# Two heads of 64 features in the two column halves of one array pass: probabilities scaled beforehand, gates turned instead of outputs

## What is computed

```python
p = jax.nn.softmax(s, axis=-1).astype(v.dtype)      # swa: with a learned sink among the logits
out = jnp.einsum('bhqs,bhsd->bhqd', p, v)           # d = 64
y = jnp.concatenate([ya * jax.nn.silu(ga), yb * jax.nn.silu(gb)], axis=-1)
x = x + y @ w_out_ab[j]
```

## Time and profile before

| | |
|---|---|
| median of 3 runs | 951.78 us (950.68 to 952.01) |
| the profiled execution, its own time | 951.7 us |
| its span in the trace | 949.9 us |
| PE busy | 936.1 us, 99% |
| PEld busy | 815.5 us, 86% |
| DVE busy | 637.9 us, 67% |
| ACT busy | 544.1 us, 57% |
| granted clock of PE over the span | 0.998 |

### The profile page before, as it was taken

One profiled execution on the slowest core, in us unless ns is written; L12 is line 12 of the kernel. 1 busy time (PEld: TensorE's weight loads), 2 busy tenths in 40 slices (PEclk: granted clock), 3 DMA queues, 4 the chain that ended last, 5 costly groups with the idle time before them and its releaser, 6 DMA issues.

```text
span 949.9 us, 14440 instructions
## 1 busy us (share of the span) xinstructions
PE 936.1 (99%) x5452; PEld 815.5 (86%) x5452; DVE 637.9 (67%) x1258; ACT 544.1 (57%) x1046; POOL 57.2 (6%) x109
## 2 busy tenths in 40 slices
PE   9999999999999999999999999999999999999997
PEld 7778788888888898989888888899988898888886
DVE  4888784877776667667666656477964767556664
ACT  6686673657676575567444444465754666444442
POOL 3001330002010030000000000000000000000000
PEclk9999999999999999999999999999999999999999
DMA  9986534554334274445556656665455256655641
GB/s 286 260 194 121 175 133 158 181 181 146 136 121 113 77 211 161 149 130 173 187 179 198 200 177 233 183 184 153 139 173 177 89 178 189 204 183 179 201 175 44
DMA packets 109584, 159.88 MB, mean 168 GB/s; under 512 B 10734, under 2 KB 45900, under 8 KB 109260
## 3 DMA queue, kind: packets, MB, share of 16 engines
q1 hardware_dynamic: 109080, 158.40, 53.7%
q10 hardware_dynamic: 436, 0.56, 0.2%
HBM read 156.32 MB, written 2.11 MB: 167 GB/s over the span
## 4 chain that ended last, share of the span: by engine, by line
PE 92%; DVE 3%; ACT 1%; issue 1%; DMA 1%; SPq 1%; DVEq 0%; ACTq 0%
PE bank L498 22%; PE bank L500 22%; PE bank L499 22%; PE bank L1206 9%; PE bank L1209 5%; PE bank L640 3%; PE bank L654 2%; PE bank L666 2%; PE bank L552 2%; DVE w_lo L1970 1%; DMA raw<-in_w_in_ab 1%; PE bank L625 1%; PE bank L1347 1%; SPq L2759 1%; DVE xT L2028 0%
## 5 line engine op out<-in xcount | busy, mean ns | idle before, releaser
L1970 DVE TENSOR_TENSOR w_lo<-raw,w_hi 128x1024 fp32r<-128x1024 f32 (+3 forms) x296 | 335.2, 1177 | 136.6 <-ACT w_hi L1425 136.1
L1425 ACT CAST w_hi<-raw 128x1024 fp32r<-128x1024 f32 (+3 forms) x296 | 282.1, 1011 | 128.2 <-DMA raw<-in_mlp_w_in 72.0
L498 PE MATMUL bank<-w_hi,xT 128*128 128x512 f32 (+1 forms) x366 | 145.2, 397 | 1.4 <-issue 0.9
L500 PE MATMUL bank<-w_hi,xT 128*128 128x512 f32 (+1 forms) x366 | 141.2, 386 | 0.0
L499 PE MATMUL bank<-w_lo,xT 128*128 128x512 f32 (+1 forms) x366 | 140.9, 385 | 0.0
L498 PE MATMUL bank<-w_hi,hT_hi 128*128 128x512 f32 (+1 forms) x348 | 136.7, 393 | 2.0 <-DVE w_lo L1970 1.7
L500 PE MATMUL bank<-w_hi,hT_lo 128*128 128x512 f32 (+1 forms) x348 | 135.0, 388 | 0.0
L499 PE MATMUL bank<-w_lo,hT_hi 128*128 128x512 f32 (+1 forms) x348 | 134.9, 388 | 0.0
L498 PE MATMUL bank<-xT,w_hi 128*128 128x256 f32 x368 | 106.0, 288 | 0.3 <-DVE w_lo L1970 0.3
L1206 PE MATMUL bank<-xT,w_hi 128*128 128x512 f32 x384 | 104.5, 394 | 0.0
L500 PE MATMUL bank<-xT,w_lo 128*128 128x256 f32 x368 | 104.1, 283 | 0.0
(11 more groups left out here) (276 smaller groups left out, 1313.7 us busy)
## 6 DMA issues: line engine op xcount, KB each, us to landing
raw<-in_mlp_w_in SPq DMA_DIRECT2D x32, 1024.0 KB, 5.2
raw<-in_mlp_w_out SPq DMA_DIRECT2D x32, 1024.0 KB, 5.1
raw<-in_w_in_ab SPq DMA_DIRECT2D x13, 1024.0 KB, 10.6
raw<-in_w_in_cd SPq DMA_DIRECT2D x13, 1024.0 KB, 5.1
raw<-in_xa_w_kv SPq DMA_DIRECT2D x8, 1024.0 KB, 5.1
raw<-in_sb_w_qkv SPq DMA_DIRECT2D x16, 512.0 KB, 5.0
raw<-in_w_out_ab SPq DMA_DIRECT2D x4, 1024.0 KB, 5.2
raw<-in_w_out_cd SPq DMA_DIRECT2D x4, 1024.0 KB, 5.1
```

Of the source, the lines that this page charges most:

```text
L498: pe.matmul(o, wh, ih, start=start, stop=False, skip_group_check=True)
L500: return pe.matmul(o, wl, ih, start=False, stop=stop, skip_group_check=True)
L1425: nc.scalar.copy(w_hi[:, u % SLOTS, a], raw[:, u % SLOTS, a]).then_inc(hi_ready, 1)
L1970: V.tensor_tensor(w_lo[:, u % SLOTS, a], raw[:, u % SLOTS, a], w_hi[:, u % SLOTS, a].bitcast(F32), ALU.subtract).then_inc(lo_ready, 1)
```

## The change

In moba, fox and swa, DVE scales the exponentials by the reciprocal of their sum in place (`normalise`, two instructions on 128 x 128 and 128 x 256 behind the reciprocal), and `turn_probs` waits for that (`norm_ready`) and no longer for the exponentials alone. `values_pair` replaces two calls of `values`: v (128 x 64) is the stationary operand, the turned probabilities are the moving one (256 and then 128 columns), and the two heads of a pair are placed in the column halves of the array by `tile_position`, so that one bank holds features by tokens for both. It stands once at the end of an iteration. The gates are turned instead of the outputs (`turn_gate`, 8 transposes for each of ga, gb and gd, the same number as before): ga at the end of fill 1 into banks 3 and 7, gb at the end of fill 11 into banks 0 and 1, gd at the start of fill 3 of swa into banks 0 and 3. ACT copies the first of the two banks back to SBUF, DVE the second (`turned_gate`). `outputs` is now one product on 128 x 256 for a pair, and ACT and DVE split its result from SBUF (`gated_hi`, `gated_lo`).

```diff
+            def values_pair(ka, kb):
+
+                g = ka["g"]
+                begin(("Y", g), 7)
+                pe.wait_ge(probsT_ready, kb["turn"])
+                places = ((ka, 0), (kb, HD))
+                for k, a in places:
+                    pe.matmul(banks[7][a:a + HD, 0:S], k["v"](0), k["pt"][:, 0:S], start=True, stop=False, tile_position=(0, a),
+                              skip_group_check=True)
+                for k, a in places:
+                    ins = pe.matmul(banks[7][a:a + HD, P:S], k["v"](1), k["pt"][:, S:S + P], start=False, stop=True, tile_position=(0, a),
+                                    skip_group_check=True)
+                end(("Y", g), ins, (gated_ready, pair_no[ka["kind"]] + ka["h"] // 2 + 1))
+                products["Y", kb["g"]] = products["Y", g]
+
+            def turn_gate(name, bs):
+
+                panel = panel_of[name]
+                for t in range(T):
+                    for one in released[name, t]:
+                        pe.wait_ge(*one)
+                for n, b in enumerate(bs):
+                    begin(("gT", name, n), b)
+                    for c in (2 * n, 2 * n + 1):
+                        for t in range(T):
+                            o = banks[b][:, (c % 2) * S + t * P:(c % 2) * S + (t + 1) * P]
+                            ins = pe.transpose(o, arena[:, panel, t * PANEL + c * P:t * PANEL + (c + 1) * P], ident[:, :])
+                    end(("gT", name, n), ins)
...
                     for n in range(2):
-                        old = ks[2 * p - 2 + n] if p else None
                         if p:
-                            turn_probs(old)
+                            turn_probs(ks[2 * p - 2 + n])
                         for f in fill.get(2 * p + n, []):
                             f()
-                        if p:
-                            values(old)
...
+                    if p:
+                        values_pair(*ks[2 * p - 2:2 * p])
...
+            def turned_gate(name):
+
+                condition(act, ("gT", name, 1))
+                ps = condition(act, ("gT", name, 0))
+                nc.scalar.copy(pan(panel_of[name], 0), ps[:, :]).then_inc(read_of(("gT", name, 0))[0], 1)
+                own.last = read_of(("gT", name, 0))
...
             def outputs(k):
 
-                recip(k)
-                g, vd = k["g"], k["vd"]
-                ps = condition(dve, ("Y", g))
-                for t in range(T):
-                    o = k["gate"](t)
-                    ins = V.scalar_tensor_tensor(out=o, in0=ps[:, t * vd:(t + 1) * vd], scalar=rsum[:, 2 * g + t:2 * g + t + 1],
-                                                 in1=o, op0=ALU.mult, op1=ALU.mult)
-                    own.sig(ins, y_ready if t == T - 1 else None)
+                o = gated_chunk(k["kind"], k["h"] // 2)
+                ps = condition(dve, ("Y", k["g"]))
+                dve.wait_ge(*read_of(("gT", {"moba": "ga", "fox": "gb", "swa": "gd"}[k["kind"]], k["h"] // 4)))
+                own.sig(V.tensor_tensor(o, ps[:, 0:S], o, ALU.mult), gated_ready)
...
-                0: [lambda: gate_finish("ga")], 1: [qk_squares("qb")], 2: [qk_rsqrt("qb")],
+                0: [lambda: gate_finish("ga")], 1: [qk_squares("qb")], 2: [qk_rsqrt("qb"), lambda: turned_gate("ga")],
```

More of the change, by code:

```diff
@@ L395, in build @@
             turns += not first_map
-            outputs += k["kind"] in ("moba", "fox", "swa") or k["kind"] == "diff" and k["c"] == 1
-            norms += k["kind"] in ("mla", "xa") or k["kind"] == "diff" and k["c"] == 1
+            outputs += k["kind"] == "diff" and k["c"] == 1
+            norms += k["kind"] in ("moba", "fox", "swa", "mla", "xa") or k["kind"] == "diff" and k["c"] == 1
             k.update(turn=turns, output=outputs, norm=norms)
@@ L454, in build @@
         row_rope = pan(11, 0)[:, S:2 * S]
-        GATE_PARTS = ((0, 2, 4, 3), (2, 1, 5, 5), (3, 1, 6, 7))
+        gate_panel_of = {"moba": 3, "fox": 7, "swa": 6}
+        gated_chunk = lambda kind, p: arena[:, gate_panel_of[kind], p * S:(p + 1) * S]
+        pair_no = {kind: 4 * n for n, kind in enumerate(("moba", "fox", "swa"))}
+        panel_of = {"qa": 0, "ka": 1, "va": 2, "ga": 3, "qb": 4, "kb": 5, "vb": 6, "gb": 7,
+                    "qc": 0, "kc": 1, "vc": 2, "gc": 3, "qd": 4, "kvd": 5, "gd": 6}
         block = ctx.enter_context(nc.Block())
@@ L646, in turn_probs @@
                 begin(("PT", g), b)
-                if k["kind"] in ("moba", "fox", "swa", "sb"):
+                if k["kind"] == "sb":
                     pe.wait_ge(probs_ready, g + 1)
@@ L891, in gate, with gate_chunks @@
                 yr[key] = gated(key, *a)
-            def gate_part(key, panel, n, ks):
-                first, chunks, b0, last = GATE_PARTS[n]
-                yr[key, n] = gated((key, n), panel, b0, ks[last]["output"], first, chunks)
+            def gate_chunks(key, chunks):
+                yr[key] = chunks_ready(state["loT"])
+                state["loT"] += chunks
             def gate_chunk(key):
@@ L1475, in hi_one, with gated_hi @@
                 own.sig(ins, hiT_ready)
+            def turned_gate(name):
[3 more added lines that the diff above has]
+                own.last = read_of(("gT", name, 0))
+            def gated_hi(kind, ps, base):
+                for p in ps:
+                    act.wait_ge(gated_ready, pair_no[kind] + p + 1)
+                    own.sig(nc.scalar.copy(xT_hi[:, base + p, :], gated_chunk(kind, p)), hiT_ready)
             def hi_T(name, chunks, dst, base=0):
@@ L1662, in _, with pairs @@
             front("qa", "ka", "va", "ga")
-            def pairs(ks, units_at, after, ahead={}, both_turned=()):
+            def pairs(ks, units_at, after, ahead={}):
                 for p in range(len(ks) // 2 + 1):
@@ L2313, in _, with pairs @@
             front("qa", "ka", "va", "ga")
-            def pairs(ks, after, late, between={}, early=()):
+            def pairs(ks, after, late, between={}):
                 for p in range(len(ks) // 2 + 1):
```

86 lines of the change are left out of this document (47 added, 39 removed).

## The result

The changed kernel takes 959.41 us (median of 6 runs, 958.15 to 960.1) where the kernel before takes 951.27 in the same series: a ratio of 1.0081, 95% interval 1.0070 to 1.0091 (the two medians alone give 1.0086). The profiled execution took 959.21 with a span of 957.4, so 7.5 more than the one before (951.7 and 949.9). The forecast was 958.4, within 954 to 964.

What follows compares the result with a forecast made beforehand. PE, busy 99% of the span, was taken to bound the kernel, with DVE and ACT mattering only where PE waits. From 951.7 us, -3.2 + 1.7 + 5.1 + 1.1 + 2.0 = +6.7 gave 958.4, range 954 to 964.

Steps and rivals of the forecast that it cites:

- values, 12 pairs: Values of two heads on PE: overlapping column halves cost 0.96 a pair instead of 1.22, saving 3.2 us over twelve.
- first wait, gate: Turning ga after fill 1: PE idles until DVE finishes the gate, about 69.2; +1.7 us.
- bank 3: 13th matmul of kb: PE waits from 74.1 to 79.2 for ACT's copy, behind head 2's exponentials; +5.1 us.
- clock: PE's clock falls to half in the 5.1 us wait and takes time to return; +2.0 us, bounds 0 and 2.7.
- later waits: Rest of the pairs and swa: 2.4 us of new waits less 1.3 given back; +1.1, bounds -2.1 and +3.5.
- the other end of the bound, 1.6: Cost in us of a pair of values if the column halves run one after the other.
- Rival 2: Column halves of the values run serially or overlap only partly: 965 us, or 961; chance 0.20.
- Rival 3: PE does not wait for bank 3, ACT's copy being over by 74.1: 951.3 us, no change; chance 0.07.
- Rival 1: PE's clock holds through the long wait: 956.4 us; chance 0.15.
- 1.3 given back: Part of PE's three longest earlier idle times in the pairs, 2.1 us together, that shrinks because PE comes later.
- Nothing on the path except where named: DVE's extra scaling and pair products, 6.6 us, were claimed to delay nothing beyond the named waits.
- Rival 4: DVE's chain sets the pace at 103 to 126, so the 5.1 us wait melts to about 2: 955; chance 0.08.

Runs made afterwards that it cites:

- e4: Changed kernel with both heads of a pair in the same column half, one after the other, second head's values left out; 965.69 us, ratio 1.0147.
- e1: Changed kernel with the two banks of turned ga swapped, so VectorE's early copy reads bank 3 and ScalarE's late one bank 7; 953.37 us, ratio 1.0018.
- e6: On top of e1, copies of turned gb and gd and the high parts of moba's and fox's outputs moved on ScalarE; 952.85 us, ratio 1.0005.
- e8: Changed kernel, banks as they were, with ScalarE's copy of bank 3 moved ahead of the exponentials of head 2; 953.09 us, ratio 1.0014.
- e2: Changed kernel with ga's banks swapped and ga turned in fill 2, behind the scores, instead of at the end of fill 1; 953.41 us, ratio 1.0017.
- e9: e7 with the 48 scalings of the probabilities left out on VectorE, so outputs lack the division by the sums; 948.22 us, ratio 0.9966.
- e5: Changed kernel with head 0 scaled before gate ga is finished, and ga turned within the kb unit into banks 7 and 6; 952.71 us, ratio 1.0017.
- e10: e7 with three pieces of VectorE's work moved: head 5's scaling, gb's second low part and a low part in swa; 950.85 us, ratio 0.9985.
- e7: Changed kernel with the edits of e5 and e6 together; 952.53 us, ratio 1.0004.
- e3: Changed kernel with idle matmuls on the identity keeping PE at work in the first two waits; 958.15 us, ratio 1.0065.

## Why the prediction was right

The time, the sign and the mechanism were right: the wait for bank 3 behind ScalarE's copy, and the clock behind it, are the larger part of the loss. That the time came out within 1 us owes something to luck, since several terms were off and in part made up for each other.

| term | forecast | in the trace |
|---|---|---|
| values, 12 pairs | -3.2 | -4.0 (0.89 for a pair, not 0.96) |
| first wait, gate | +1.7 | +1.9 |
| bank 3 | +5.1 | +3.3 |
| clock | +2.0 | +3.4, of which 1.7 make the 5.1 into 3.3 |
| later waits | +1.1 | +3.3 |
| sum | +6.7 | +7.9, the profiled executions differ by 7.5 |

*Values.* The row halves were the right row to take the price from, and the other end of the bound, 1.6, is where e4 goes, with 1.54. (Twelve times 0.26 is 3.1, not 3.2.) The Trainium skill's rule (TensorE: Matmul & The Clock Gate, "The mechanism") by which a weight load overlaps running matmuls only in another row group did not decide here: the two column halves share their row group, and their records start 6 to 7 ns apart (90.498 and 90.505, 90.765 and 90.771). The trace before had already shown that the rule does not hold as worded: in a unit every matmul uses the whole array, and the next weight load starts 2 to 4 ns behind the start of a matmul of 390 ns (70.438 behind 70.434), which is how PE could be busy for 936.1 and PEld for 815.5 of 949.9. Rival 2 is out.

*First wait.* Right in size (1.56 to 1.91 in the traces of e1, e6, e8 and the changed kernel) and place, incomplete in cause: e2 shows that the probabilities of head 0 would have held PE as long. "Nothing on DVE ahead of it changes" was true, and still the scaling behind it had become something PE waits for.

*Bank 3.* The step from the earlier trace rows to 79.2 came out at 79.28. e1 and e8 undo it in two ways, each with the same 6 us. Rival 3 had its condition right (the copy over before the 13th matmul) but it is not what the order does. Nor was its price, 951.3: with the wait cut to 0.62 and no loss of clock e1 takes 953.4, because the later waits are longer than forecast.

*Clock.* Rival 1 is out. That it would fall with the long wait was right, though it fell 0.95 behind its end and not in it, and cost 1.6 to 1.7 where 2.0 was forecast; that it fell behind the first one too was not foreseen, and was free.

*Later waits.* This is the term that was mis-sized. From 85 to 320 PE's idle times over 0.15 sum to 2.9 before and 6.2 after. The step "1.3 given back" held, with 1.4 (1.08 and 0.18 are gone, 0.35 is 0.19). The new ones are 1.25 for the scaled probabilities near 134, which the walk did not have at all; 1.48 for the values of heads 10 and 11, where I had 0.45, since I counted the copy of the gate but not the four high parts behind it; 1.18 in swa (forecast 1.1; the view names `w_lo`, but ScalarE's copy of bank 0 ended 0.1 ahead, and e6, which moves that copy, takes the wait away); 0.43 at the end of fox (forecast 0.85); and 0.34 more for a `w_lo`. The sentence that failed is "Nothing on the path except where named" on VectorE's 6.6 us. VectorE's busy time rose by 9.4, and e9 shows that the scalings alone cost some 3.4 to 4.3 once PE is no longer held elsewhere.

*Rival 4* (the wait is paid back) did not happen in the changed kernel, as the constant 6.4 between its matmuls and those of e1 shows. It showed in the repaired kernels: e5 takes two waits of 2.2 away and gets 0.7 (0.2 between the two traces). What stays open is how the rest splits between ScalarE's order and VectorE's load in swa, where the wait of 1.1 moved in e6 and hardly shrank in e10; no run changed it alone. The change also brings three weight units (the second of the cross attention, "oab" 0 and "oab" 1) one step forward on ScalarE (two of them on VectorE too) and drops an exception in the order of swa; what these moves alone cost, no run shows.

## What to carry to other kernels

When an edit gives a bank a new reader, look at what stands ahead of that reader on its own engine, and give the bank that is needed first to the engine that comes to it first: here this was a swap of two numbers and 6 us. Work taken off a busy engine and put on one with a quarter free is not free while the two hand each other work every few microseconds: the 4.0 that the pairs gained on PE came back almost whole as waits for VectorE and ScalarE, and changing VectorE's order gave less than 1 of it back in the trace. And when a wait is removed, read the next one in the same chain before counting the gain, because two pieces of work on one engine may hold the same instruction, and only the later shows. Where a wait is near the length at which the clock sometimes falls, look at the clock of every execution before trusting a median: by their mean clock, about half of e6's executions lost it and half did not.

## What was not expected of the hardware

- Column halves of the array overlap as row halves do: 96 records of 64-column matmuls took 12.6 us in two halves and 20.0 in one.
- The clock does not follow the length of the last idle time alone. It fell behind idle times of 1.91 (changed kernel, half from 70.0) and 1.89 (e6), and each time only 0.7 to 0.8 after PE had begun to work again; it held through 1.88 (e2), 1.89 (e5 and e7, near 105), 1.70 (e8) and 1.56 (e1), each in the one execution that was profiled. I have no experiment that tells what else counts.
- A loss of clock may cost nothing: the 1.7 lost between 70.0 and 73.4 lay in front of a wait whose end ScalarE set, and keeping the clock full in e3 brought that matmul no earlier.
- Weight loads of the whole array run beside matmuls of the whole array: PE 936.1 and PEld 815.5 busy of 949.9.
